# Gates and NSA product of a merge stage as seven block products on 512 columns

## The reference

```python
gm = jax.nn.sigmoid(g_merge.reshape(B, S, N_BRANCH, D_MODEL))      # g_merge: 3 x 1024 columns of h @ w_in
y = (gm[:, :, 0] * (y_nsa @ w_proj_nsa[l]) + gm[:, :, 1] * (y_ml @ w_proj_ml[l])
     + gm[:, :, 2] * (y_mem @ w_proj_mem[l]))
x = x + rmsnorm(y @ w_out[l], g_post_mix[l])
h = rmsnorm(x, g_pre_ffn[l])
gate, up = (h @ w_ffn_in[l])[..., :D_FF], (h @ w_ffn_in[l])[..., D_FF:]
x = x + rmsnorm((jax.nn.silu(gate) * up) @ w_ffn_down[l], g_post_ffn[l])
```

## Time and profile before

| | us |
|---|---|
| median of 3 runs | 1713.23 (1712.73 to 1713.35) |
| the profiled execution, whole | 1711.17 |
| its span, first to last instruction | 1709.3 |
| busy in the span: PE, PEld | 1362.2, 767.4 |
| busy: DVE, ACT, POOL | 443.3, 188.3, 38.9 |
| merge, first to last matmul of it | 1319.63 to 1461.10 |
| product with w_out_2 | 1461.65 to 1489.36 |

### The profile page before, as it was taken

The page is one execution under the profiler, slowest core; times in us unless marked ns, Lnnn a source line. Parts: engine busy times, 40 slices in busy tenths (PEclk is TensorE's granted clock), DMA queues, the critical chain, the costliest instruction groups (busy, mean ns, idle before and its releaser), DMA issues.

```text
span 1709.3 us, 20156 instructions
## 1 busy us (share of the span) xinstructions
PE 1362.2 (80%) x8248; PEld 767.4 (45%) x8248; DVE 443.3 (26%) x951; ACT 188.3 (11%) x503; POOL 38.9 (2%) x104
## 2 busy tenths in 40 slices
PE   9998566765766665766576668999998999999997
PEld 5553121121212111311131113687777888599953
DVE  2432011111101110110011011334454010367875
ACT  2320010000000000000000001223343000100000
POOL 1100000000000000000000000000000000000000
PEclk9999888788789888988898778999999999999999
DMA  9668999999999999999999999122250345334332
GB/s 401 248 247 351 433 429 428 435 425 434 430 428 433 430 432 427 434 429 430 432 431 430 428 436 416 41 78 75 103 209 28 123 158 235 148 135 161 115 142 87
DMA packets 31041, 517.81 MB, mean 303 GB/s; under 512 B 3472, under 2 KB 4496, under 8 KB 6928
## 3 DMA queue, kind: packets, MB, share of 16 engines
q1 hardware_dynamic: 29072, 514.01, 71.9%
q10 hardware_dynamic: 1920, 3.10, 0.5%
HBM read 515.53 MB, written 1.05 MB: 302 GB/s over the span
## 4 chain that ended last, share of the span: by engine, by line
PE 52%; DMA 42%; DVE 4%; issue 1%; ACT 1%; SPq 0%; POOL 0%; ACTq 0%; PEldq 0%; DVEq 0%
PE ps L949 51%; DMA ring<-in_experts 41%; DVE scr L1721 1%; DVE turned_T L1608 1%; PE ps L1340 1%; ACT xn L820 0%; DMA vecs<-in_vecs 0%; PE ps L955 0%; DVE scr L1835 0%; PE ps L1039 0%; ACT scr L826 0%; DVE x L2001 0%; DVE gains L1999 0%; DVE ps L1833 0%; PE ps L1015 0%
## 5 line engine op out<-in xcount | busy, mean ns | idle before, releaser
L949 PE MATMUL ps<-ring,scr 128*32 128x512 f32 (+1 forms) x3066 | 488.8, 767 | 263.9 <-DMA ring<-in_experts 259.2
L949 PEld LDWEIGHTS ps<-ring,scr 128*32 128x32 f32 (+1 forms) x3066 | 123.3, 137 | 603.7 <-issue 311.9
L949 PE MATMUL ps<-turned_T,ring 128*128 128x128 f32 (+1 forms) x1952 | 318.8, 324 | 7.2 <-DVE turned_T L1608 2.8
L949 PEld LDWEIGHTS ps<-turned_T,ring 128*128 128x128 f32 x1952 | 287.8, 191 | 35.2 <-issue 9.9
L949 PE MATMUL ps<-ring,turned_T 128*128 128x128 f32 (+3 forms) x576 | 156.4, 430 | 2.0 <-DVE turned_T L1608 2.0
L949 PE MATMUL ps<-scr 128*128 128x512 f32 (+9 forms) x668 | 136.9, 409 | 18.5 <-DVE scr L1721 13.0
L949 PEld LDWEIGHTS ps<-ring,turned_T 128*128 128x128 f32 x576 | 94.4, 191 | 60.6 <-issue 46.5
L949 PEld LDWEIGHTS ps<-scr 64*128 64x128 f32 (+4 forms) x668 | 68.9, 173 | 82.9 <-issue 47.1
L1724 DVE TENSOR_TENSOR x<-x,ps 128x512 f32<-128x512 f32 x64 | 44.0, 688 | 209.3 <-PE ps L949 209.3
L1716 DVE SCALAR_TENSOR_TENSOR scr<-scr,ps 128x512 f32<-128x512 f32 x16 | 11.0, 688 | 294.6 <-PE ps L949 294.6
L1714 DVE SCALAR_TENSOR_TENSOR scr<-scr,ps 128x512 f32<-128x512 f32 x16 | 11.0, 688 | 226.5 <-ACT scr L739 226.5
(11 more groups left out here) (283 smaller groups left out, 863.1 us busy)
## 6 DMA issues: line engine op xcount, KB each, us to landing
ring<-in_experts SPq DMA_DIRECT2D x70, 4096.0 KB, 22.7
ring<-in_experts SPq DMA_DIRECT2D x48, 2048.0 KB, 21.1
ring<-in_w_ffn_in SPq DMA_DIRECT2D x11, 2048.0 KB, 7.7
ring<-in_w_merge SPq DMA_DIRECT2D x8, 1536.0 KB, 6.3
ring<-in_w_ffn_down SPq DMA_DIRECT2D x11, 1024.0 KB, 4.8
ring<-in_w_out SPq DMA_DIRECT2D x4, 2048.0 KB, 23.7
ring<-in_w_ml SPq DMA_DIRECT2D x4, 2048.0 KB, 7.9
ring<-in_w_nsa SPq DMA_DIRECT2D x4, 2048.0 KB, 7.8
```

Source lines behind the costliest of these rows:

```text
L949: return pe.matmul(o, l, rr, start=start, stop=stop)
```

## The change

The merge works on two quads of 512 output columns, straight-line code without a loop. Each quad has five strips of 2 MB: gate 0, NSA, gate 1, both short branches, gate 2. Gates and NSA product are done as in the FFN: `merge_sevens` on TensorE, `differences`, `merge_sums` and `merge_blocks` on VectorE; the short branches go directly (`merge_direct`), 16 matmuls of 256 columns each. Results are put together in SBUF (`gG`, `pG`, `yG`), tanh is taken there. The sums live in slot 4 (which no strip uses until the FFN) and in scratch, in turn. The first strip is loaded, its sums made and `hT`'s differences taken before the groups. `MERGE_SLOTS` gives each strip's slot; w_out_2 is loaded after the third strip. The host packs the new strips.

```diff
+MERGE_SLOTS = [3, 2, 5, 3, 2, 5, 2, 3, 5, 2]
+GATES0, NSA, GATES1, BOTH, GATES2 = range(5)
...
-        thG = G(2 * 768, "p (u n) -> p u n", u=2)
-        yG = G(2 * 768, "p (u n) -> p u n", u=2)
+        sG = [slot[TAIL[4]].rearrange("p (q k n) -> p q k n", q=4, k=4), G(SLOT, "p (q k n) -> p q k n", q=4, k=4)]
+        tY = G(4 * 512, "p (q k t) -> p q k t", q=4, k=4)
+        gG, pG, yG = (G(1024) for _ in range(3))
+        u2G, u3G = (G(T, "p (f n) -> p f n", f=2) for _ in range(2))
+        tH = scr[:, AHEAD + SLOT - 4 * 512:AHEAD + SLOT].rearrange("p (q k t) -> p q k t", q=4, k=4)
...
             r.load(2, whole(2, "w_cmp", 0, tslot))
+            def merge_strip(n):
+                r.load(MERGE_SLOTS[n], whole(MERGE_SLOTS[n], "w_merge", n, tslot))
+            merge_strip(0)
+            r.count(4, 0)
             with sp.Fori(0, GROUPS) as g:
                 r.enter(g, {0: (1, 1), 1: (1, 1), 5: (1, 1)})
                 r.load(0, whole(0, "w_ml", g, tslot))
...
                 r.load(1, whole(1, "w_memq", g, tslot))
                 r.leave(GROUPS)
-            with sp.Fori(0, 4) as i:
-                r.enter(i, {s: (1, 1) for s in (2, 3, 4, 5)})
-                for u in range(2):
-                    r.load(2 + 2 * u, whole(2 + 2 * u, "w_merge", i * 2 + u, tslot))
-                    r.load(3 + 2 * u, whole(3 + 2 * u, "w_proj", i * 2 + u, tslot))
-                r.leave(4)
+            merge_strip(1)
+            merge_strip(2)
             r.load(0, whole(0, "w_out_2", 0, tslot))
             r.load(1, whole(1, "w_out_2", 1, tslot))
+            for n in range(3, 10):
+                merge_strip(n)
             for s in range(FF_STEPS):
                 r.load(FF_SLOTS[s % 4], whole(FF_SLOTS[s % 4], "w_ffn_in", s, tslot))
...
-            with act.Fori(0, 4) as i:
-                for u in range(2):
-                    m = i * 2 + u
-                    act.wait_ge(mg_free, m + 1)
-                    act.wait_ge(mg_ps, m + 1)
-                    act.activation(thG[:, u, 0:512], bank[4 * u], ACT.Tanh, scale=0.5)
-                    act.activation(thG[:, u, 512:768], bank[4 * u + 1][:, 0:T], ACT.Tanh, scale=0.5)\
-                       .then_inc(mg_th, 1)
+            for n in range(6):
+                quad, b = divmod(n, 3)
+                act.wait_ge(mg_sb, 4 * quad + (1, 3, 4)[b])
+                act.activation(gG, gG, ACT.Tanh, scale=0.5).then_inc(mg_th, 1)
...
-            pe.wait_ge(ynsa_done, 8)
-            pe.wait_ge(yml_done, 4)
-            pe.wait_ge(ymem_done, 4)
-            with pe.Fori(0, 4) as i:
-                r.enter(i, {s: (1, 1) for s in (2, 3, 4, 5)})
-                for u in range(2):
...
-
-            pe.wait_ge(mg_free, 9)
+            half_bank = lambda b0, q: bank[b0 + q // 2][:, (q % 2) * T:(q % 2 + 1) * T]
+            def merge_arrived(n):
+                r.arrived(MERGE_SLOTS[n], 1)
+                merge_landed[n] = r.incs[MERGE_SLOTS[n]]
+            def merge_sevens(quad, c, src, tt, frees):
+                n, u = 5 * quad + c, 4 * quad + (0, 1, 2, None, 3)[c]
+                b0 = 4 if c == NSA else 0
+                b = src.rearrange("p (j k) (t n) -> p j t k n", j=2, t=NT)
+                w = tstrip[MERGE_SLOTS[n]].rearrange("p (j k) (i n) -> p j i k n", j=2, i=2)
+                sums = sG[u % 2]
+                merge_arrived(n)
+                for q, (l, rr) in enumerate(((w[:, 0, 0], b[:, 0, 0]), (w[:, 1, 0], b[:, 1, 0]),
+                                             (sums[:, 1], tt[:, 1]), (sums[:, 0], tt[:, 0]), (sums[:, 3], b[:, 1, 1]),
+                                             (sums[:, 2], tt[:, 2]), (w[:, 1, 1], tt[:, 3]))):
+                    if q == 2:
+                        pe.wait_ge(mg_sum, u + 3 if u else 2)
+                    for f in range(2):
+                        for k in range(4):
+                            ins = mm(half_bank(b0, q)[:, f * P:(f + 1) * P], l[:, k, f * P:(f + 1) * P], rr[:, k, :],
+                                     k == 0, k == 3)
+                            if frees is not None and (q, f, k) == (0, 0, 0):
+                                ins.then_inc(tfree[frees], 1)
+                    if q in (1, 3, 5, 6):
+                        ins.then_inc(mg_ps, 1)
+            def merge_direct(quad, c, src, frees):
+                w = tstrip[MERGE_SLOTS[5 * quad + BOTH]][:, 4 * c:4 * c + 4, :]
+                for m in range(4):
+                    for k in range(4):
+                        ins = mm(bank[4 + m][:, 0:T], w[:, k, m * P:(m + 1) * P], src[:, k, :], k == 0, k == 3)
+                        if m == 0 and k < len(frees):
+                            ins.then_inc(tfree[frees[k]], 1)
+                    if c == 1 or m == 3:
+                        ins.then_inc(mp_ps, 1)
+            for quad in range(2):
+                s = MERGE_SLOTS[5 * quad:5 * quad + 5]
+                if quad:
+                    pe.wait_ge(mg_sb, 4)
+                merge_sevens(quad, GATES0, hT, tH, MERGE_SLOTS[BOTH] if quad else None)
+                if quad:
+                    pe.wait_ge(mg_free, 5)
+                else:
+                    pe.wait_ge(ynsa_done, 8)
+                    r.count(4, 0)
+                merge_sevens(quad, NSA, yT, tY, s[GATES0])
+                pe.wait_ge(mg_sb, 4 * quad + 1)
+                merge_sevens(quad, GATES1, hT, tH, s[NSA])
+                merge_arrived(5 * quad + BOTH)
+                pe.wait_ge(mg_sb, 4 * quad + 2)
+                merge_direct(quad, 0, yml, [s[GATES1], 4] if quad else [s[GATES1]])
+                pe.wait_ge(mg_sb, 4 * quad + 3)
+                merge_sevens(quad, GATES2, hT, tH, None)
+                pe.wait_ge(mg_free, 5 * quad + 1)
+                merge_direct(quad, 1, ymem, [s[GATES2]])
             r.arrived(0, 1)
             r.arrived(1, 1)
+            pe.wait_ge(mg_sb, 8)
             for t in range(NT):
                 for h in range(2):
                     for k in range(KC):
-                        if (t, h, k) == (0, 0, KC - 1):
-                            pe.wait_ge(mg_free, 10)
+                        if (t, h) == (0, 0) and k > 3:
+                            pe.wait_ge(mg_free, 3 + k)
                         ins = mm(bank[2 * t + h], yT2[:, k, t * P:(t + 1) * P], tstrip[h][:, k, :], k == 0, k == KC - 1)
+                        if (t, h, k) == (0, 0, 0):
+                            ins.then_inc(tfree[MERGE_SLOTS[5 + BOTH]], 1)
                     ins.then_inc(out2_ps, 1)
...
+            def differences(tt, src):
+                b = src.rearrange("p (j k) (t n) -> p j t k n", j=2, t=NT)
+                chain(dve.tensor_tensor(tt[:, 0], b[:, 0, 1], b[:, 0, 0], ALU.subtract))
+                chain(dve.tensor_tensor(tt[:, 1], b[:, 1, 1], tt[:, 0], ALU.subtract))
+                dve.tensor_tensor(tt[:, 2], b[:, 1, 1], b[:, 0, 1], ALU.subtract)
+                return dve.tensor_tensor(tt[:, 3], b[:, 1, 0], tt[:, 1], ALU.subtract)
+            def merge_sums(n, u):
+                w = tstrip[MERGE_SLOTS[n]].rearrange("p (j k) (i n) -> p j i k n", j=2, i=2)
+                o = sG[u % 2]
+                dve.wait_ge(tfull[MERGE_SLOTS[n]], merge_landed[n])
+                chain(dve.tensor_tensor(o[:, 0], w[:, 0, 1], w[:, 1, 1], ALU.add))
+                chain(dve.tensor_tensor(o[:, 1], o[:, 0], w[:, 0, 0], ALU.subtract))
+                dve.tensor_tensor(o[:, 2], w[:, 0, 0], w[:, 0, 1], ALU.subtract)
+                dve.tensor_tensor(o[:, 3], w[:, 1, 0], o[:, 1], ALU.subtract).then_inc(mg_sum, 1)
             dve.memset(kvc[:, 4, :], 0.0)
             dve.memset(hidv, 0.0)
...
             dve.tensor_copy(kvc[:, 4, 0:CMP_L], peT[:, :]).then_inc(pe_sb, 1)
+            dve.wait_ge(hT_done, 20)
+            differences(tH, hT).then_inc(mg_sum, 1)
             dve.wait_ge(if_ps, 1)
             chain(dve.tensor_scalar(iR, bank[5][0:4, 0:T], ifb[0:4, 0:1], None, ALU.add))
             chain(dve.tensor_scalar(fR, bank[5][0:4, T:2 * T], ifb[0:4, 1:2], None, ALU.add))
...
                               const("eye4", 4).unsqueeze(2).broadcast_to([4, 4, T]), ALU.mult).then_inc(st_sb, 1)
+            merge_sums(GATES0, 0)
             dve.wait_ge(cmp_ps, 1)
...
             dve.wait_ge(ynsa_done, 8)
             dve.wait_ge(yml_done, 4)
-            dve.memset(nt_[:, 34:35], 0.0).then_inc(mg_free, 2)
-            with dve.Fori(0, 4) as i:
-                chain.enter(i, 6)
...
-                chain.leave(4)
+            differences(tY, yT).then_inc(mg_sum, 1)
+            merge_sums(NSA, 1)
+            def merge_total(o, q, p, more=None):
+                ins = dve.tensor_tensor(o, p, q, ALU.add)
+                if more is None:
+                    chain(ins)
+                else:
+                    ins.then_inc(more, 1)
+            def merge_blocks(u, dst, b0):
+                o = dst.rearrange("p (i f t n) -> p i t f n", i=2, f=2, t=NT)
```

(99 more changed lines are left out.)

## The result

The median fell from 1712.98 us (4 runs, 1712.38 to 1713.35) to 1696.70 (4 runs, 1696.55 to 1698.22): ratio 0.9902, interval 0.9887 to 0.9918, 16.3 us less, against a forecast of 1698.1 in 1696.0 to 1703.0. The profiled execution took 1696.55, its span 1694.8.

The account below looks back on a forecast made before the run. TensorE time alone bounds the merge: 143.1 us before less 127.9 after saves 15.2, so the profiled execution falls from 1711.2 to 1696.0; with the median 2.1 above, 1698.1 us, range 1696 to 1703.

Parts of the forecast that it names:

- 127.9 us for the merge and 15.2 of gain: Merge on TensorE: 100.1 us of block products plus 27.8 direct, against 143.1 before with seams and start.
- The unit's 12.51 us from the FFN loop: Merge's gate and NSA units: each 56 matmuls of 128 columns take the FFN loop's unit period, 12.51 us.
- The rival that 128-column matmuls run worse here: Merge on TensorE, rival 3: weight loads show, 326 ns per matmul instead of 223, kernel 1744 us; chance 0.02.
- The 2.7% of the prediction: FFN loop on TensorE: a 128-column matmul takes 2.7% more per column than a 256-column one, 223.4 against 217.5.
- 139.24 us / 320 = 435 ns each: Merge before the change: 320 TensorE matmuls of 256 columns, priced at 435 ns each.
- seams and start: Merge before: three seams of 0.74 us, one of 0.55, and 1.10 us at the start, all expected to go.
- Slack at the third gate: Merge, both quads: second gate is recombined on VectorE 1.2 us before TensorE needs it, the narrowest wait.
- the second quad's NSA unit: Merge: TensorE waits there for the first quad's last sum, ready at 74.1, needed at 76.5 us, slack 2.4.
- Rivals 1 and 2: Merge strips land late: 11 us gives 1703 (rival 1, 0.08); from 14.4 the gain is lost (rival 2, 0.02).
- Rival 4: Before the groups: moved VectorE work is not hidden, up to 8 us back, 1706 us; chance 0.02.
- rival 5: After the merge: something there was the real limit, so no gain; unseen loss of the gain was given 0.03.
- Nothing here touches what makes it so: Whole kernel: the median stays 2.1 us above the profiled execution, taking 1696.0 to 1698.1.

Follow-up runs that it names:

- e5: Changed kernel, NSA strip's slot freed by the 33rd matmul of the second gate's unit, 7.15 us later, both quads: 1715.03 us, 1.0019 of the kernel before.
- e6: Changed kernel, hT's differences and first gate's sums moved from before the groups to behind the last group operation: 1698.08 us, 0.9911 of the kernel before.

## Why the prediction was right

1. **TensorE's time.** Forecast 127.9 us for the merge and 15.2 of gain, measured 127.8 and 15.4. The unit's 12.51 us from the FFN loop held to 0.01 us in every unit but the first, which took 12.61. The rival that 128-column matmuls run worse here is out: they cost 3.5% more per column than 256-column ones (223.4 against 215.9), not half as much again. (The 2.7% of the prediction came from the 435 ns, which is too high, see 2.) The Trainium skill's rule on streams at 128 columns (TensorE: Matmul & The Clock Gate, Back-to-back issue gap), by which they take half as much again as the bare streaming, doesn't hold for this float32 stream.
2. **The split of the gain.** The term that was mis-sized is "139.24 us / 320 = 435 ns each": that mean holds the hidden part of each turn's drained wait, 34.81 us for 80 matmuls that take 34.54 in an unbroken stream. With 432 ns the block products are worth 10.5 us, not 11.3, and seams and start 5.0, not 3.9. The two errors nearly cancel in the sum, and not by luck: the merge before was read from start to start (1319.63 to 1461.65), whatever one matmul in it takes, and the 435 ns enters the new time only with the 64 direct matmuls, 0.2 us.
3. **The waits.** Slack at the third gate forecast 1.2 us, measured 1.5 and 1.7: what follows the third and the fourth sum starts 1.14 us after it, not 1.26, so that the four take 4.8 and not 5.04. At the second quad's NSA unit it was 3.1 (last sum written at 1392.73, unit from 1395.82), forecast 2.4. ScalarE's tanh took 1.06 us, not 1.15. No wait bit, in either quad.
4. **Rivals 1 and 2** were priced at one to one beyond the slack. The wait is, but a stop of 2 us may and one of 6 us did cost 1.7 to 1.9 us more by the clock. With both third gates 7.15 us late, the whole gain was gone (e5, 1.0019), where the prediction's price, 2 x (7.15 - 1.2) = 11.9 us, left 3.3.
5. **Rival 4**, lost cover before the groups, did not occur, and e6 shows that the placement hardly mattered. Nor did rival 5: from the start of the product with w_out_2 to the end of the span lie 247.65 us in both kernels (1709.3 - 1461.65 and 1694.8 - 1447.15).
6. **From the profiled execution to the median.** "Nothing here touches what makes it so" carried 2.1 us over to the new median. The changed kernel's profiled execution stands at its median (1696.55 and 1696.70), so the 2.1 belonged to that one execution of the kernel before, and the forecast was high by 1.95 for it. The profiled execution in turn came 0.55 over the forecast 1696.0, mainly since its stages ahead of S ended 0.9 us later than in the trace before, which leaves 1.4. Traces differ by such amounts in the expert stage, and by 1.6 where the kvc piece runs in 9.04 us for 7.41; which of them it was in the unprofiled runs stays open.

## What to carry to other kernels

Where a loop elsewhere in the same kernel already does what a change brings in, take the period of its unit and not the durations of its matmuls, and walk every cross-engine wait through one turn of the new order: that gave a 128 us stage to 0.1 us and named the one narrow wait. Trading a tenth of a saturated TensorE's columns for 60 us of idle VectorE took 7.6% off TensorE's time (10.5 of 138.2 us; the rest of the tenth went into the 3.5% more per column). VectorE's work cost nothing as long as no wait bit, but a wait that bites can cost more than its length, because the clock can fall behind it, as it did behind both stops of e5. Look at the last turn of a software-pipelined loop too: its empty slots hold the first products of the next stage.
